# Seven block products in place of eight for five gate and up tile pairs of each feed-forward block

## The chip, the cores and the metric

The kernel runs on one core of a Trainium2 chip. The metric is the device time of the whole program in microseconds (us), the median of several executions; the profile shown is of one execution. TensorE is called PE here, VectorE DVE, ScalarE ACT, GpSimd POOL and SyncE SP.

## The reference

Two layers, each of a feed-forward network, a mixer (a recurrent group beside latent attention) and a second feed-forward network, over T = 528 tokens (16 meta tokens and 512 others) of 1024 features, all in 32 bit floats. The part that the change touches is the first half of the feed-forward network, D_FF = 2816:

```python
def swiglu(u, w_gate, w_up, w_down):
    return (jax.nn.silu(u @ w_gate) * (u @ w_up)) @ w_down
...
    for l in range(DEPTH):
        f = swiglu(rms_norm(h, ffn1_pre_g[l]), ffn1_w_gate[l], ffn1_w_up[l], ffn1_w_down[l])
        h = h + 0.5 * rms_norm(f, ffn1_post_g[l])
        ...
        f = swiglu(rms_norm(h, ffn2_pre_g[l]), ffn2_w_gate[l], ffn2_w_up[l], ffn2_w_down[l])
        h = h + 0.5 * rms_norm(f, ffn2_post_g[l])
    return h[:, N_META:]
```

## The kernel before

Features lie on the 128 partitions, tokens along the free axis. The program is six blocks, b = 0 to 5: blocks 0, 2, 3 and 5 are feed-forward blocks, 1 and 4 mixers. A feed-forward block has 22 pairs m, each of one gate tile and one up tile (128 columns of w_gate or w_up, 8 chunks of 128 rows: 128x1024 numbers), and then 8 output chunks of two w_down tiles (128x1408).

To keep 32 bit accuracy every operand is split into a high part (rounded to fp32r) and the rest: xh and xl of the tokens, whi and wlo of a weight tile. A product of a chunk is three matmuls, xh by whi, xl by whi, xh by wlo (`tile`, L1590), each once per half of the tokens (264 columns). A gate or up tile is thus 8 x 3 x 2 = 48 matmuls. In block 5 the meta tokens are no longer needed, and a tile from the pair m = 2 on is 24 matmuls of 512 columns.

A weight tile n goes through a ring of four places. SP loads it to `raw` once the low part of tile n - 4 has been made; ACT rounds it to `whi` (`hi`, L741) once PE has used tile n - 4; POOL subtracts (`lo`, L677, four instructions of 256 columns) to give `wlo`; PE waits for that (`slot_in`, L1600). Each engine works through its instructions in the order in which the code writes them.

The product of a tile stands in one of four pairs of PSUM banks, one bank for each half of the tokens; the pairs are taken in turn. For each m, `hidden` on DVE (L1297) scales the gate product from PSUM (L1301) and the up product (L1304), multiplies with the silu that ACT has made (L1308) and makes the low part of the hidden value (L1311); `hidden` on ACT (L913) makes the silu (L920), the high part of the hidden value (L924) and, between them, `hi` of two later tiles. Before the pair m = 0 stands a seam, in which the residual, the norm and xh, xl of the block are made, and `opening` on PE (L1618) takes the first three tiles half by half. The pairs are written as loops (`Fori`) on every engine.

Of the kernel before, what the change touches and what calls it, by code (L numbers as in the profile page):

```python
# [28 lines left out]
ALU = mybir.AluOpType  # L29
# [88 lines left out]

def build_program(nc, a, out, depth, d_ff):
# [6 lines left out]

    tiles = []
    slot0 = []
    for b in range(NB):
        slot0.append(len(tiles))  # L130
        tiles += MIX_TILES if b % 3 == 1 else [DC] * (2 * FC) + [FH] * (2 * DC)
    NSLOT = len(tiles)

# [5 lines left out]
    for b in range(NB):  # L139
        U[b, "post"] = U[b, "pre"] = n  # L140
        n += 1
        parts = MIX_UNITS if b % 3 == 1 else dict(gu=2 * FC, out=DC)
        for name, k in parts.items():
            U[b, name] = n
            n += k
    U[NB, "post"] = n

# [55 lines left out]
    def lo_made(n):  # L203

        return n + 1 + RING

# [21 lines left out]
    def out_slot(b, m):  # L228

        return slot0[b] + (S_OUT + m if b % 3 == 1 else 2 * FC + 2 * m + 1)  # L230
# [14 lines left out]
    with ExitStack() as ctx:  # L245
# [41 lines left out]
        hidl = sb_at("hidl", arena + FC * CH, [P, FC, T], F32R)  # L287

# [159 lines left out]
        lo_ready = sem("lo_ready")  # L448
        slots_used = sem("slots_used")
# [134 lines left out]

        def block_of(j):

            return (0, N_META) if j == 0 else (N_META + (j - 1) * P, P)
# [8 lines left out]
        def _(sp):  # L596
            def load(n, src, adv=0):

                sp.wait_ge(lo_ready, n + 1 + adv)
                k = tiles[n] * P  # L600
                sp.dma_start(raw[:, n % RING, 0:k], src).then_inc(raw_full[n % RING], 16)
# [20 lines left out]
            for b in range(NB):  # L622
                l, s0 = b // 3, slot0[b]
                if b % 3 == 1:
# [21 lines left out]
                    with sp.Fori(0, DC // 4) as j:  # L646
                        for m in range(4):
                            load(s0 + S_OUT + m, a["w_out"][l, j * 4 + m], j * 4)
                else:
# [3 lines left out]
                    with sp.Fori(1 if b == 0 else 0, FC // 2) as j:  # L653
                        for m in range(2):
                            load(s0 + 2 * m, a[name + "_gate"][l, j * 2 + m], j * 4)
                            load(s0 + 2 * m + 1, a[name + "_up"][l, j * 2 + m], j * 4)
                    with sp.Fori(0, DC // 2) as j:
                        for m in range(2):
                            for q in range(2):
                                load(s0 + 2 * FC + 2 * m + q, a[name + "_down"][l, j * 2 + m, q], j * 4)  # L660
# [15 lines left out]
        def _(pool):  # L676
            def lo(n, adv=0):  # L677

                pool.wait_ge(hi_ready, n + 1 + adv)
# [6 lines left out]

            def lo_run(first, last):

                n = first
                while n < last:  # L690
                    k = n
                    while k < last and tiles[k] == tiles[n] and (k in ARENA) == (n in ARENA):
                        k += 1
                    rounds = (k - n) // RING
                    if rounds > 1 and n not in ARENA:
                        with pool.Fori(0, rounds) as j:
                            for m in range(RING):
                                lo(n + m, j * RING)
                        n += rounds * RING
                    while n < k:  # L700
                        lo(n)
                        n += 1
# [15 lines left out]
            for b in range(NB):  # L718
                if b == 0:
                    pool.wait_ge(lo_ready, lo_made(RING - 2))  # L720
# [3 lines left out]
                lo_run(slot0[b] + RING, slot0[b + 1] if b + 1 < NB else NSLOT)  # L724
# [7 lines left out]
        def _(act):  # L732
# [8 lines left out]
            def hi(n, adv=0):  # L741
                if n < NSLOT:
                    r, k = n % RING, tiles[n] * P

                    if n in PREV:
                        act.wait_ge(slots_used, slot_used(PREV[n]) + adv)
                    act.wait_ge(raw_full[r], 16 * (n // RING + 1) + adv * 4)
# [161 lines left out]
            def ffn(b):  # L909
# [3 lines left out]
                def hidden(m, it=0):  # L913

                    adv = it * RING
                    ug = u0 + 2 * m
                    mm = m + 2 * it

                    act.wait_ge(psum_free[pair_of(ug)], read_out(ug) + it)
                    nc.scalar.activation(toks(tmp[2], trim), toks(tmp[0], trim), ACT.Silu).then_inc(silu_ready, 1)  # L920
                    if m > 0:
                        hi(s0 + 2 * m + RING, adv)
                    act.wait_ge(hid_ready, f0 + mm + 1)
                    nc.scalar.activation(toks(hidh[:, mm, :], trim), toks(tmp[3], trim),  # L924
                                         ACT.Copy).then_inc(hidh_ready, 1)
                    hi(s0 + 2 * m + 1 + RING, adv)

                hidden(0)
                hidden(1)
                with act.Fori(0, FC // 2 - 2) as j:  # L930
                    hidden(2, j)
                    hidden(3, j)
                hidden(FC - 2)
                hidden(FC - 1)
# [199 lines left out]
        def _(dve):  # L1134
# [96 lines left out]
            def first_seam():  # L1231

                def low(n, part):
# [3 lines left out]
                    else:  # L1237
                        dve.wait_ge(hi_ready, n + 1)
                    nc.vector.tensor_tensor(wlo[:, n, at], raw[:, n, at], whi[:, n, at].bitcast(F32), ALU.subtract)\  # L1239
                        .then_inc(first_lo if part == 0 else lo_ready, 1)  # L1240
# [52 lines left out]
            def ffn(b):  # L1293
# [3 lines left out]
                def hidden(m, it=0):  # L1297
                    adv, mm = it * RING, m + 2 * it
                    ug, uu = u0 + 2 * m, u0 + 2 * m + 1
                    dve.wait_ge(slots_used, slot_used(s0 + 2 * m) + adv)  # L1300
# [774 lines left out]
```

## Time and profile before

| | us |
|---|---|
| median of 3 runs | 2030.61 (2030.28 to 2030.77) |
| the profiled execution | 2030.33 |
| its span in the trace | 2028.5 |
| PE busy, matmuls | 2014.0 (99%) |
| PE busy, weight loads | 1927.0 (95%) |
| DVE busy | 697.2 (34%) |
| ACT busy | 747.9 (37%) |
| POOL busy | 997.4 (49%) |

The span is the time from the first to the last instruction that the profile shows; the execution's own time is 1.83 us more. Busy shares are means over stages that differ. Matmuls are pipelined: the time of one from start to end is over twice the time from one start to the next, so what a matmul costs is read from the distance of starts, not from its duration. Some matmul records can be missing.

### The profile page before, as it was taken

The numbers are of one execution on the slowest core, as the hardware profiler recorded it, in microseconds if no ns is written. First come the engines' busy times: TensorE is split into PE (matmuls) and PEld (weight loads), VectorE is DVE, ScalarE is ACT, GpSimd is POOL, SyncE is SP. The second block draws the span as 40 slices with busy tenths as digits, with TensorE's granted clock in tenths as the row PEclk, the third lists the DMA queues.
The fourth block names the chain that finished last, engine by engine and source line by source line (L and its number), as shares of the span: only waits on it lengthen the run. The fifth ranks groups of instructions, "written<-read, shape, count | busy, mean of one in ns | idle before, by whom it ended". The sixth has DMA issues, their size and how long they took to land.

```text
span 2028.5 us, 37353 instructions
## 1 busy us (share of the span) xinstructions
PE 2014.0 (99%) x15084; PEld 1927.0 (95%) x15084; DVE 697.2 (34%) x1093; ACT 747.9 (37%) x1210; POOL 997.4 (49%) x1257
## 2 busy tenths in 40 slices
PE   9999999999999999999999999999999999999998
PEld 8999999999899999999999999999998998888887
DVE  6222210378546222210062222103885462222102
ACT  5222222455556222232252222223555462232221
POOL 3544454475315544454374444544853155554542
PEclk9999999999999999999999999999999999999999
DMA  4322332222101322232122323321222013323321
GB/s 175 103 85 92 98 111 83 69 94 79 63 32 45 106 89 93 85 125 88 57 94 84 93 87 100 113 84 58 96 84 67 32 53 104 97 92 111 114 72 42
DMA packets 48415, 174.85 MB, mean 86 GB/s; under 512 B 5184, under 2 KB 9408, under 8 KB 48320
## 3 DMA queue, kind: packets, MB, share of 16 engines
q1 hardware_dynamic: 48176, 173.40, 26.1%
q8 instruction: 71, 1.16, 0.2%
q14 instruction: 24, 0.20, 0.0%
q10 hardware_dynamic: 144, 0.10, 0.0%
HBM read 171.38 MB, written 2.10 MB: 86 GB/s over the span
## 4 chain that ended last, share of the span: by engine, by line
PE 98%; DVE 1%; ACT 0%; DMA 0%; issue 0%; SPq 0%; DVEq 0%
PE ps L1588 97%; PE ps L1927 1%; DMA h<-in_x 0%; DVE osb L1535 0%; DVE xl L1545 0%; DVE tail_step L1205 0%; PE ps L1806 0%; ACT xh L778 0%; DVE probT L1503 0%; ACT prob L1061 0%; DVE small L1512 0%; DVE h L1210 0%; ACT tmp L1097 0%; ACT xh L1112 0%; DVE wlo L1239 0%
## 5 line engine op out<-in xcount | busy, mean ns | idle before, releaser
L683 POOL TENSOR_TENSOR wlo<-raw,whi 128x256 fp32r<-128x256 f32 (+2 forms) x1148 | 911.9, 826 | 787.4 <-ACT whi L748 787.4
L1588 PE MATMUL ps<-xh,whi 128*128 128x264 f32 (+2 forms) x3000 | 706.1, 298 | 3.2 <-DVE xl L1244 1.3
L1588 PE MATMUL ps<-xl,whi 128*128 128x264 f32 (+2 forms) x3000 | 703.0, 297 | 0.0
L1588 PE MATMUL ps<-xh,wlo 128*128 128x264 f32 (+2 forms) x3000 | 701.6, 297 | 0.0
L1588 PEld LDWEIGHTS ps<-xh,whi 128*128 128x128 f32 x3000 | 489.1, 188 | 21.0 <-DVE wlo L1239 2.3
L1588 PEld LDWEIGHTS ps<-xl,whi 128*128 128x128 f32 x3000 | 487.8, 188 | 14.8
L1588 PEld LDWEIGHTS ps<-xh,wlo 128*128 128x128 f32 x3000 | 487.5, 188 | 14.0
L748 ACT ACTIVATE whi<-raw 128x1024 fp32r<-128x1024 f32 (+2 forms) x289 | 321.4, 1114 | 152.5 <-PE ps L1588 152.4
L1588 PE MATMUL ps<-hidh,whi 128*128 128x264 f32 (+2 forms) x1276 | 313.6, 296 | 0.0
L1588 PE MATMUL ps<-hidh,wlo 128*128 128x264 f32 (+2 forms) x1276 | 312.3, 295 | 0.0
L1588 PE MATMUL ps<-hidl,whi 128*128 128x264 f32 (+2 forms) x1276 | 312.3, 295 | 0.0
L1588 PEld LDWEIGHTS ps<-hidl,whi 128*128 128x128 f32 x1276 | 214.2, 188 | 6.2
L1588 PEld LDWEIGHTS ps<-hidh,wlo 128*128 128x128 f32 x1276 | 213.8, 188 | 5.9
L1588 PEld LDWEIGHTS ps<-hidh,whi 128*128 128x128 f32 x1276 | 213.2, 188 | 6.1
L924 ACT ACTIVATE hidh<-tmp 128x528 f32 (+3 forms) x88 | 56.6, 643 | 412.7 <-DVE tmp L1308 412.7
L1304 DVE TENSOR_TENSOR tmp<-ps,rs_in 128x528 f32<-128x528 f32 (+1 forms) x88 | 61.9, 703 | 407.4 <-PE ps L1588 407.4
L1283 DVE TENSOR_TENSOR tmp<-tmp,tmp 128x264 f32<-128x264 f32 (+3 forms) x52 | 36.3, 698 | 413.5 <-ACT tmp L811 360.2
L920 ACT ACTIVATE tmp<-tmp 128x528 f32<-128x528 f32 (+1 forms) x88 | 56.6, 643 | 264.9 <-DVE tmp L1301 264.8
L1301 DVE TENSOR_TENSOR tmp<-ps,rs_in 128x528 f32<-128x528 f32 (+1 forms) x88 | 61.9, 704 | 218.7 <-PE ps L1588 203.8
L716 POOL TENSOR_TENSOR tmp<-tmp,tmp 128x264 f32<-128x264 f32 (+1 forms) x55 | 45.8, 833 | 103.1 <-ACT tmp L785 100.4
L1311 DVE TENSOR_TENSOR hidl<-tmp,hidh 128x528 f32 (+3 forms) x88 | 63.7, 723 | 80.9 <-ACT hidh L924 80.9
L683 POOL TENSOR_TENSOR w_mix<-raw,w_mix 128x256 fp32r<-128x256 f32 x32 | 25.5, 829 | 106.5 <-ACT w_mix L748 106.5
(192 smaller groups left out, 1685.9 us busy)
## 6 DMA issues: line engine op xcount, KB each, us to landing
raw<-in_ffn_up SPq DMA_DIRECT2D x88, 512.0 KB, 3.5
raw<-in_ffn_down SPq DMA_DIRECT2D x64, 704.0 KB, 4.1
raw<-in_ffn_gate SPq DMA_DIRECT2D x87, 512.0 KB, 3.5
raw<-in_w_in SPq DMA_DIRECT2D x28, 512.0 KB, 3.5
raw<-in_w_out SPq DMA_DIRECT2D x16, 512.0 KB, 3.5
raw<-in_w_q SPq DMA_DIRECT2D x8, 384.0 KB, 3.3
out_t<-h SPq DMA_DIRECT2D x16, 128.0 KB, 1.7
h<-in_x SPq DMA_DIRECT2D x2, 528.0 KB, 5.1
```

The source lines that it names most:

```text
L683: ins = nc.gpsimd.tensor_tensor(w_lo(n)[:, at], raw[:, r, at], w_hi(n)[:, at].bitcast(F32), ALU.subtract)
L716: nc.gpsimd.tensor_tensor(hs, hs, square_of(k, s, trim), ALU.add)\
L748: nc.scalar.activation(w_hi(n)[:, 0:k], raw[:, r, 0:k], ACT.Copy).then_inc(hi_ready, 1)
L920: nc.scalar.activation(toks(tmp[2], trim), toks(tmp[0], trim), ACT.Silu).then_inc(silu_ready, 1)
L924: nc.scalar.activation(toks(hidh[:, mm, :], trim), toks(tmp[3], trim), ACT.Copy).then_inc(hidh_ready, 1)
L1283: nc.vector.tensor_tensor(acc, acc, part(tmp[m % 2], trim), ALU.add).then_inc(sum_ready, 1)
L1301: nc.vector.tensor_tensor(halves(tmp[0], trim), unit(ug, trim, trim and m > 1), halves(rs_in, trim), ALU.mult).then_inc(psum_free[pair_of( ...
L1304: nc.vector.tensor_tensor(halves(tmp[1], trim), unit(uu, trim, trim and m > 0), halves(rs_in, trim), ALU.mult).then_inc(psum_free[pair_of( ...
L1311: nc.vector.tensor_tensor(toks(hidl[:, mm, :], trim), toks(tmp[3], trim), toks(hidh[:, mm, :], trim).bitcast(F32), ALU.subtract).then_inc( ...
L1588: return nc.tensor.matmul(o, w, x, start=start, stop=stop)
L1927: ins = nc.tensor.transpose(ps[:, c0:c0 + P], prob[e % 4][:, k0:k0 + P], ident)
```

## The change

For m = 5, 7, 9, 11 and 13 of each feed-forward block the gate tile G and the up tile U are taken together as a 2 x 2 matrix of blocks: rows gate and up, columns the lower and the upper four chunks of features; the tokens as a 2 x 2 matrix too, lower and upper features by first and second half of the tokens (B11, B12 / B21, B22). The product takes eight block products (four chunks by 264 tokens) in the kernel before; the change takes seven, by Winograd's form of Strassen's identity. In place of two weight tiles there are four in the ring: the gate as it is; `s13`, the sums S1 = Ur + Ul (r and l the upper and lower chunks) and S3 = Gl - Ul; `s2up`, S2 = S1 - Gl beside Ur; `s4`, S4 = Gr - S2, half a tile. DVE makes the sums in `raw` (L1443 to L1461 of the new kernel) from the two loaded tiles, ACT rounds each as before, and the low parts of the last three are made by DVE, those of the gate and of all other tiles by POOL.

The token sums T1 = B12 - B11, T2 = B22 - T1, T3 = B22 - B12, T4 = B21 - T2 are the same for all five pairs and are made once per block, while PE works on m = 1 to 4: for each of four chunks ACT scales two chunks of h to `t_in`, DVE makes four sums (`t_sums`), ACT rounds them to `t_hi` and DVE makes `t_lo` (128x1056 each). They lie where hidden values of later m will stand.

A changed pair uses three PSUM pairs: z, the gate's and the up's. ACT copies the first block product from z to SBUF (`part_copy`), so that its bank can be used again, and DVE adds the seven products up (`strassen_sums`, six additions of 264 columns). The loops over tiles are written out on all engines.

```diff
+STRASSEN = (5, 7, 9, 11, 13)
...
+            if m in STRASSEN:
+                for i, kind in enumerate(("gate", "s13", "s2up", "s4")):
+                    KIND[n + i] = kind
+                tiles += [DC, DC, DC, KH]
...
+    LO_DVE = {0, 1, 2} | {n for n in KIND if KIND[n] != "gate"}
...
+        def raw_reusable(eng, n):
+            if n >= RING:
+                wait_lo(eng, n - RING)
+                if KIND.get(n - RING) in ("gate", "s2up"):
+                    eng.wait_ge(w_sums, 3 * STRASSEN_N[n - RING] + 3)
```

On ACT:

```diff
+                for m in range(FC):
+                    n = TILES_OF[b, m]
+                    if m in STRASSEN:
+                        part_copy(m)
+                        for i in range(3):
+                            hi(n[i] + RING)
+                        silu(m)
+                        hi(n[3] + RING)
+                        hid_hi(m)
+                        continue
+                    silu(m)
+                    if m:
+                        hi(n[0] + RING)
+                    if m == 1:
+                        sum_hi(0)
+                        sum_inputs(1)
+                    hid_hi(m)
+                    hi(n[1] + RING)
+                    if 0 < m < 4:
+                        sum_hi(m)
+                    if m < 3 and m != 1:
+                        sum_inputs(0 if m == 0 else 3)
+                    elif m == 1:
+                        sum_inputs(2)
```

On DVE (`strassen_sums` is cut to its first three additions):

```diff
+                    if part == 0:
+                        dve.wait_ge(part_copied, q + 1)
+                        dve.wait_ge(slots_used, slot_used(n[0]))
+                        nc.vector.tensor_tensor(c11, x, c11, ALU.add).then_inc(part_added, 1)
+                    elif part == 1:
+                        dve.wait_ge(part_added, 6 * q + 1)
+                        dve.wait_ge(part_mm, 2 * q + 2)
+                        nc.vector.tensor_tensor(x, x, bank(z, trim, 1), ALU.add).then_inc(part_added, 1)
+                        dve.wait_ge(part_added, 6 * q + 2)
+                        dve.wait_ge(slots_used, slot_used(n[1]))
+                        nc.vector.tensor_tensor(y, x, bank(z, trim, 0), ALU.add).then_inc(psum_free[pair_of(z)], 1)
...
+                for m in range(FC):
+                    n = TILES_OF[b, m]
+                    nxt = [i + RING for i in n]
+                    sums(nxt[0])
+                    if m in STRASSEN:
+                        strassen_sums(m, 0)
+                        sums(nxt[1])
+                        low(nxt[0])
+                        sums(nxt[2])
+                        low(nxt[1])
+                        strassen_sums(m, 1)
+                        strassen_sums(m, 2)
+                        low(nxt[2])
+                        strassen_sums(m, 3)
+                        gate(m)
+                        up(m)
+                        sums(nxt[3])
+                        hid(m)
+                        low(nxt[3])
+                        hid_lo(m)
+                        continue
+                    gate(m)
+                    if m == 1:
+                        t_sums(0)
+                    elif 2 <= m <= 4:
+                        t_low(m - 1)
+                    sums(nxt[1])
+                    low(nxt[0])
+                    up(m)
+                    hid(m)
+                    low(nxt[1])
+                    hid_lo(m)
+                    if m == 1:
+                        t_low(0)
+                    if 1 <= m <= 3:
+                        t_sums(m)
+                    if b == 0 and m == FC - 4:
+                        decay_rates()
```

On PE, in `strassen`; `part` runs over four chunks k, three matmuls each:

```diff
+                        mm(o, wh, xhk, k == 0, False)
+                        mm(o, wh, xlk, False, False)
+                        ins = mm(o, wl, xhk, False, k == KH - 1)
...
+                slot_in(n[0])
+                part(n[0], False, tokens(0, a0), bank(z, trim, 0), ug).then_inc(part_mm, 1)
+                part(n[0], True, tokens(1, a0), bank(ug, trim, 0), uu).then_inc(slots_used, 1)
+                slot_in(n[1])
+                pe.wait_ge(t_lo_ready, KH * (b // 3 * 2 + b % 3 // 2) + KH)
+                part(n[1], False, sums(0), bank(uu, trim, 1))
+                pe.wait_ge(part_copied, q + 1)
+                part(n[1], True, sums(2), bank(z, trim, 0)).then_inc(slots_used, 1)
+                slot_in(n[2])
+                part(n[2], False, sums(1), bank(z, trim, 1)).then_inc(part_mm, 1)
+                part(n[2], True, sums(3), bank(uu, trim, 0)).then_inc(slots_used, 1)
+                slot_in(n[3])
+                part(n[3], False, tokens(1, a1), bank(ug, trim, 1), following).then_inc(slots_used, 1)
```

On PE, in the first changed pair of block 0: the last chunk of the second block product, and the beginnings of the two products of tile `s13` (a row is one matmul).

```order
L1803 MATMUL ps<-xh,whi 128x264 [waits psum_free1]
L1803 MATMUL ps<-xl,whi 128x264
L1803 MATMUL ps<-xh,wlo 128x264
L1803 MATMUL ps<-t_hi,whi 128x264 [waits t_lo_ready,lo_dve]
L1803 MATMUL ps<-t_lo,whi 128x264
...
L1803 MATMUL ps<-t_hi,wlo 128x264
L1803 MATMUL ps<-t_hi,whi 128x264 [waits part_copied]
L1803 MATMUL ps<-t_lo,whi 128x264
L1803 MATMUL ps<-t_hi,wlo 128x264
```

Twelve matmuls by token sums stand between the wait for `t_lo` and the wait for ACT's copy; from there the next product goes into the bank that was copied.

On ACT, one of the two pairs in the body of the loop before: silu, `hi`, high part of the hidden value, `hi`.

```order
L920 ACTIVATE tmp_67<-tmp_65 128x528 [waits psum_free3]
L746 REGISTER_ALU
L748 ACTIVATE whi<-raw 128x1024 [waits raw_full2,slots_used]
L923 REGISTER_ALU
L924 ISA [waits hid_ready]
L924 ACTIVATE hidh<-tmp_68 128x528
L746 REGISTER_ALU
L748 ACTIVATE whi<-raw 128x1024 [waits raw_full3,slots_used]
```

And in the kernel after, from the end of pair m = 4 to the end of m = 5 of block 0.

```order
L970 ACTIVATE tmp_67<-tmp_65 128x528 [waits psum_free1]
L799 ACTIVATE whi<-raw 128x1024 [waits w_sums,slots_used]
L974 ACTIVATE hidh<-tmp_68 128x528 [waits hid_ready]
L799 ACTIVATE whi<-raw 128x512 [waits w_sums,slots_used]
L998 ACTIVATE tmp_69<-ps 128x264 [waits part_mm]
L799 ACTIVATE whi<-raw 128x1024 [waits raw_full2,slots_used]
L799 ACTIVATE whi<-raw 128x1024 [waits raw_full3,slots_used]
L799 ACTIVATE whi<-raw 128x1024 [waits raw_full0,slots_used]
L970 ACTIVATE tmp_67<-tmp_65 128x528 [waits psum_free0]
L799 ACTIVATE whi<-raw 128x1024 [waits w_sums,slots_used]
L974 ACTIVATE hidh<-tmp_68 128x528 [waits hid_ready]
```

The copy from PSUM (L998) stands behind two `hi` and the high part of the hidden value of m = 4, and ahead of the three `hi` for the tiles that follow the changed pair.

On DVE, one of the two pairs in the body of the loop before.

```order
L1301 TENSOR_TENSOR tmp_65<-ps,rs_in 128x528 [waits slots_used]
L1303 REGISTER_ALU
L1304 TENSOR_TENSOR tmp_66<-ps,rs_in 128x528 [waits slots_used]
L1306 REGISTER_ALU
L1307 REGISTER_ALU [waits psum_free0]
L1308 TENSOR_TENSOR tmp_68<-tmp_67,tmp_66 128x528 [waits silu_ready]
L1311 ISA [waits hidh_ready]
L1311 TENSOR_TENSOR hidl<-tmp_68,hidh 128x528
```

And in the kernel after, from the scaling of the gate of m = 4 (L1395) to that of m = 5.

```order
L1395 TENSOR_TENSOR tmp_65<-ps,rs_in 128x528 [waits slots_used]
L1436 TENSOR_TENSOR t_lo<-t_sum,t_hi 128x1056 [waits t_hi_ready]
L1460 TENSOR_TENSOR raw<-raw 128x512 [waits w_sums,lo_ready]
L1468 TENSOR_TENSOR wlo<-raw,whi 128x1024 [waits hi_ready]
L1403 TENSOR_TENSOR tmp_66<-ps,rs_in 128x528 [waits slots_used]
L1411 TENSOR_TENSOR tmp_68<-tmp_67,tmp_66 128x528 [waits silu_ready,psum_free2]
L1468 TENSOR_TENSOR wlo<-raw,whi 128x512 [waits hi_ready]
L1416 TENSOR_TENSOR hidl<-tmp_68,hidh 128x528 [waits hidh_ready]
L1481 TENSOR_TENSOR ps<-tmp_69,ps 128x264 [waits slots_used,part_copied]
L1485 TENSOR_TENSOR tmp_69<-tmp_69,ps 128x264 [waits part_mm,part_added]
L1488 TENSOR_TENSOR tmp_69<-tmp_69,ps 128x264 [waits slots_used,part_added]
L1490 TENSOR_TENSOR tmp_69<-tmp_69,ps 128x264 [waits psum_free3]
```

Between the scaling of the gate and of the up product (L1395 and L1403) now stand the low part of token sums, a weight sum (L1460) and a low part of weights (L1468); behind them another low part and then the additions.

## Rows read from the trace of the kernel before

**Rows 1.** The page: span, and busy time by engine (share of it).

```profile
span 2028.5 us, 37353 instructions
...
PE 2014.0 (99%) x15084; PEld 1927.0 (95%) x15084; DVE 697.2 (34%) x1093; ACT 747.9 (37%) x1210; POOL 997.4 (49%) x1257
```

**Rows 2.** Waits of PE, the longest: waited for, us in total, times, longest.

```profile
PE ps L1585 <- DVE maskb L1136: 1.9, 1, 1.9
```

**Rows 3.** Timeline of DVE in block 2: start, us, instruction, [idle before <- releaser].

```profile
690.80 0.71 DVE L1301 TENSOR_TENSOR tmp<-ps,rs_in 128x528 f32<-128x528 f32 x1 [2.68 <-PE ps L1588]
...
708.42 0.71 DVE L1304 TENSOR_TENSOR tmp<-ps,rs_in 128x528 f32<-128x528 f32 x1 [5.17 <-PE ps L1588]
709.25 0.71 DVE L1308 TENSOR_TENSOR tmp<-tmp,tmp 128x528 f32<-128x528 f32 x1
...
796.52 0.71 DVE L1301 TENSOR_TENSOR tmp<-ps,rs_in 128x528 f32<-128x528 f32 x1 [2.66 <-PE ps L1588]
```

**Rows 4.** Timeline of DVE in block 5, where matmuls have 512 columns.

```profile
1678.52 0.69 DVE L1301 TENSOR_TENSOR tmp<-ps,rs_in 128x512 f32<-128x512 f32 x1 [2.11 <-PE ps L1588]
...
1711.88 0.69 DVE L1301 TENSOR_TENSOR tmp<-ps,rs_in 128x512 f32<-128x512 f32 x1 [2.39 <-PE ps L1588]
```

**Rows 5.** Timeline of PE in the openings of blocks 3 and 5.

```profile
1035.81 0.28 PE L1588 MATMUL ps<-xh,wlo 128*128 128x264 f32 x1
...
1042.39 0.29 PE L1588 MATMUL ps<-xh,wlo 128*128 128x264 f32 x1
...
1650.36 0.28 PE L1588 MATMUL ps<-xl,whi 128*128 128x256 f32 x1
...
1656.87 0.28 PE L1588 MATMUL ps<-xh,wlo 128*128 128x256 f32 x1
```

**Rows 6.** Timeline of PE in a mixer, and of ACT in the output of block 0.

```profile
423.79 0.28 PE L1588 MATMUL ps<-xh,wlo 128*128 128x264 f32 x1
...
439.82 0.41 PE L1588 MATMUL ps<-xh,wlo 128*128 128x264 f32 x2
...
300.83 0.61 ACT L811 ACTIVATE tmp<-ps 128x528 f32<-128x528 f32 x1 [6.65 <-PE ps L1588]
...
316.89 0.61 ACT L811 ACTIVATE tmp<-ps 128x528 f32<-128x528 f32 x1 [6.65 <-PE ps L1588]
```

**Rows 7.** Timeline of PE and ACT in block 2, at the end of a pair.

```profile
708.22 0.41 PE L1588 MATMUL ps<-xh,whi 128*128 128x264 f32 x2
...
710.10 0.65 ACT L924 ACTIVATE hidh<-tmp 128x528 f32 x1 [5.21 <-DVE tmp L1308]
710.65 1.05 ACT L748 ACTIVATE whi<-raw 128x1024 fp32r<-128x1024 f32 x1
```

**Rows 8.** Groups by form: line, engine, shapes, count | busy us, mean ns | idle before.

```profile
L826 ACT ACTIVATE f_mix<-ps,par 128x264 f32<-128x264 f32 x16 | 7.6, 477 | 0.0
...
L1187 DVE TENSOR_TENSOR tmp<-f_ffn,ps 128x264 f32<-128x264 f32 x48 | 19.7, 421 | 33.9 <-ACT ps L836 33.7
L1239 DVE TENSOR_TENSOR wlo<-raw,whi 128x1024 fp32r<-128x1024 f32 x2 | 2.4, 1222 | 0.5 <-ACT whi L748 0.5
L1239 DVE TENSOR_TENSOR wlo<-raw,whi 128x512 fp32r<-128x512 f32 x2 | 1.4, 692 | 0.5 <-ACT whi L877 0.5
```

**Rows 9.** Timeline of DVE and POOL, at the start of block 3 and in block 2.

```profile
1045.22 0.71 DVE L1301 TENSOR_TENSOR tmp<-ps,rs_in 128x528 f32<-128x528 f32 x1 [3.46 <-ACT rs_in L797]
...
1051.77 1.29 DVE L1308 TENSOR_TENSOR tmp<-tmp,tmp 128x528 f32<-128x528 f32 x1
...
1056.90 0.71 DVE L1301 TENSOR_TENSOR tmp<-ps,rs_in 128x528 f32<-128x528 f32 x1 [1.98 <-PE ps L1588]
...
1049.67 6.55 POOL L683 TENSOR_TENSOR wlo<-raw,whi 128x256 fp32r<-128x256 f32 x8 [2.62 <-ACT whi L748]
...
704.96 2.81 POOL L683 TENSOR_TENSOR wlo<-raw,whi 128x256 fp32r<-128x256 f32 x4 [2.10 <-ACT whi L748]
```

**Rows 10.** DMA issues: source, engine, count, size, us to landing.

```profile
raw<-in_ffn_up SPq DMA_DIRECT2D x88, 512.0 KB, 3.5
```

More of the change, by code:

```diff
@@ L645, in _ @@
                             sp.dma_start(ropet[0][:, :], a["rope"][0]).then_inc(rope0_in, 16)
-                    with sp.Fori(0, DC // 4) as j:
-                        for m in range(4):
-                            load(s0 + S_OUT + m, a["w_out"][l, j * 4 + m], j * 4)
+                    for m in range(DC):
+                        load(s0 + S_OUT + m, a["w_out"][l, m])
                 else:
@@ L685, in lo @@
                 ins.then_inc(lo_ready, 1)
[L687 to L702, printed above, removed]
             def seam(b):
@@ L723, in _ @@
                     seam(b)
-                lo_run(slot0[b] + RING, slot0[b + 1] if b + 1 < NB else NSLOT)
+                for n in range(slot0[b] + RING, slot0[b + 1] if b + 1 < NB else NSLOT):
+                    if n not in LO_DVE:
+                        lo(n)
             for i, k in enumerate(POOL_TAIL):
@@ L925, in hidden, with sum_inputs @@
                                          ACT.Copy).then_inc(hidh_ready, 1)
[L926 to L934, printed above, removed]
+                def sum_inputs(k):
+                    if k:
+                        act.wait_ge(t_sum_ready, KH * F + k)
+                    for i in range(2):
+                        c = k + i * KH
+                        ins = nc.scalar.activation(toks(t_in[:, i, :], trim), toks(h[:, c, :], trim), ACT.Copy,
+                                                   scale=col(g, b // 3, c))
+                    ins.then_inc(t_in_ready, 1)
@@ L1723, in ffn @@
                 product(u0 + 3, s0 + 3, tin, leads=True)
-                with pe.Fori(0, FC // 2 - 1) as j:
-                    for m in range(4):
-                        product(u0 + 4 + m, s0 + 4 + m, tin, adv=j * RING, it=j, led=True, leads=True)
+                for m in range(2, FC):
+                    n, following = TILES_OF[b, m], FIRST_U[b, m + 1]
+                    if m in STRASSEN:
+                        strassen(b, m, tin, following)
+                    else:
+                        product(GATE_U[b, m], n[0], tin, led=True, leads=True)
+                        product(UP_U[b, m], n[1], tin, led=True, leads=True, lead=following)
                 output(b, [(hidh[:, k, :], hidl[:, k, :]) for k in range(FC)])
```

259 lines of the change are left out of this document (198 added, 61 removed).

## The prediction

> **What bounds the kernel now.** I read the page first: PE is busy 99% of the span the other engines under 50% [rows 1]. Then the waits of PE: even the longest is only 1.9 us, once, for a mask made at the program's start [rows 2]. So the gate and up stretches run at the pace of the matmuls, and a matmul less is worth one distance between starts. That is read on DVE, which scales the gate product once per pair: 690.80 to 796.52 us are nine pairs, 11.747 us each, 96 matmuls at 0.1224 us [rows 3]. In block 5 three pairs take 1678.52 to 1711.88 us, 11.12 each, 48 matmuls of 512 columns at 0.2317 us [rows 4].
>
> **What it removes.** A changed pair is 7 products x 4 chunks x 3 = 84 matmuls in place of 96; in block 5, 84 of 256 columns in place of 48 of 512. The pattern of a changed pair, one token half after the other with three matmuls per chunk, stands already in the openings: 54 steps in 6.58 us, 0.1219 us each at 264 columns, and 55 steps in 6.51 us, 0.1184 at 256 [rows 5]. So halving the columns of block 5 costs little: two of 256 cost 0.2368 against 0.2317 for one of 512.
>
> A changed pair has nine waits on PE (four tiles, token sums, the copy, three PSUM leads) where two tiles had four. What a wait that is met costs isn't shown alone. From above: 48 matmuls of the pairs take 5.87 us, and 48 in the output, where 132 take 16.06 us [rows 6], would take 5.84; the 0.03 us may be the two waits of a tile, 0.017 each, or nothing. I take 0.017, five more being 0.08 us a pair; below, 0.
> - Blocks 0, 2, 3, 15 pairs: 84 x 0.1219 + 0.08 = 10.32 us, so 1.43 less each, 21.4 us.
> - Block 5, 5 pairs: 84 x 0.1184 + 0.08 = 10.03, so 1.09 less each, 5.5 us.
>
> Together 26.9 us, if nothing on PE waits longer.
>
> **What it adds, and what hides it.** I call X the start of PE's first matmul of a changed pair. From the end of an ordinary pair in block 2: PE goes on at 708.22, DVE's up at 708.42, hid at 709.25 [rows 3], ACT's high part at 710.10 and its next at 710.65 [rows 7]; that is X + 0.2, 1.03, 1.88, 2.43. Next on ACT is now `hi` of s4, 512 columns, about as long as the high part of 528: 0.65 us, the next starting after 0.55 [rows 7]. So the copy from PSUM starts at X + 2.98 and, at 0.48 us (the scaled copy of 264 columns) [rows 8] and 0.1 us for the signal, is known to PE at about X + 3.55. PE wants it after 36 matmuls, X + 4.39 (X + 4.26 in block 5). This is the tightest hand-over: 0.8 us to spare. Queued behind it on ACT are the three `hi` of the next tiles, which PE needs from X + 10.3.
>
> The first of them can round at X + 3.5 to 4.5, POOL makes its low part in 2.8 us [rows 9], so it is ready by X + 7.5. The next waits for its ring place (X + 5.9) and is ready at X + 10.2, wanted at X + 16.2; the following gate at X + 13, wanted at X + 22.
>
> DVE adds six times, about 0.42 us each as the instruction of 264 columns with one operand in PSUM [rows 8]; the last can start after the pair, X + 10.5. Then gate, up, two sums into s13 (0.69 each), hid, a low part (1.22) and hidl: done near X + 17. The ordinary pair brings two sums, the gate and the low part of s2up, done near X + 21.4; up falls due at X + 22.2. So DVE enters the next changed pair with 0.8 us to spare, and is busy some 14 us of 22 (six additions 2.5, eight old instructions 5.7, four sums 2.8, three low parts 3.1), against 5.7 in two pairs before. A late DVE delays up, hid, ACT and the copy in this order, so PE waits only when DVE is more than 0.8 + 0.8 = 1.6 us late. PSUM: each pair of banks is read 5 us or more before PE wants it, z's of the next changed pair 11 us.
>
> SP: a load now also waits for the sums that read its place. The up tile of the next changed pair is loaded when POOL has made a low part at X + 7.4 and lands 3.5 us later [rows 10], X + 11; DVE wants it at X + 12.2. The bytes are the same. POOL makes three low parts in two pairs where it made four; it was no bound.
>
> Token sums, once per block beside m = 1 to 4: in block 3, from DVE's first gate at 1045.22 and its third at 1056.90 (PE's own pace) [rows 9], PE begins m = 5 at 1056.90 + 5 x 5.87 = 1086.2. DVE has to do until then four pairs (10.6 us at 0.66), 16 sums (1.8 us per chunk of four alone, up to 3.8 with POOL in the way), four low parts of 1056 columns (1.25), and 6.5 us for the weights and the gate of m = 4: 29 to 37 us in 41, with waits for ACT in between. Laid out by hand in queue order, the token sums' last low part ends at 1084 (wanted X + 2.9 = 1089) and the low part of s2up at 1086. Just in time: I take a stall of 0, and up to 3 us a block as the upper end.
>
> The port: DVE's hid took 1.29 us where POOL was subtracting and 0.71 otherwise [rows 3, 9]. The Trainium skill, "SBUF — State Buffer", in its section on which instructions contend, says that a DVE instruction with two SBUF inputs and a GpSimd one that reads SBUF lock each other out for a whole instruction; the trace agrees (1.29 = 0.71 + most of one POOL instruction of 0.70). By that rule the new weight and token sums can each lose 0.6 us beside POOL, the six additions (one operand in PSUM) nothing. It bears on the two sums into s13 at X + 12.2, where POOL runs until X + 13, and on the token sums, as counted above. Near X itself POOL rests, since both tiles that come are DVE's.
>
> The loops written out: I take 0. The mixer, already written out, has 131 matmuls of 264 columns in 16.03 us [rows 6], 0.1224 each, just the pace of the loops. "Runtime: NRT & Kernel Launch" in the Trainium skill, on instruction fetch, says that a taken branch breaks the sequential prefetch and can stall; by it the ten iterations of four blocks would give time back. The trace shows no such stall.
>
> The decay rates, small DVE instructions once in the program, move to m = 18 of block 0, where DVE idles 5.17 us before up and 2.68 before gate in each pair [rows 3]: nothing.
>
> **Sum.** 2028.5 - 26.9 = 2001.6 us of span, 2003.4 us with the 1.83 us around it. The median of the runs is 0.28 above the profiled execution: **2003.7 us**. Own range of this case: 2001.5 (no cost of waits, steps of 0.1217) to 2006.5.
>
> **Rivals.**
> - *Late preparation* (chance 0.17). The token sums and the first weight sums end after X in each block, by 2 to 3 us above the margin. For it: DVE has 29 to 37 us of work in 41, twice it waits for ACT per chunk. Against it: the margin of 1.6 us. Four blocks x 1 to 3 us: 2007 to 2015.
> - *Hand-over in each changed pair* (0.09). The copy comes late again and again, as DVE's work between the pairs runs beside POOL. 0.2 to 1.3 us x 20: 2008 to 2030.
> - *Slower* (0.04). The same place with a price above 26.9 / 20 = 1.34 us a pair. It needs DVE 1.6 + 1.34 = 2.9 us later than laid out, five instructions with 0.58 us lost each (1.29 against 0.71). Only the two sums into s13 and what follows them to X + 13 can meet POOL, by my layout; if POOL runs later than I think, low parts and sums of the next ordinary pair do too. From there 2031 to 2040.
> - *More than forecast* (0.05). Branches or register instructions of the loops cost PE something that goes: 0.065 us a pair (96 matmuls at 0.1224 against 0.1217) in all 88 pairs, 5.7 us: 1997 to 2001.
> - *Not seven products in effect* (0.01). If a matmul of the new order did not overlap its weight load as in the openings, the pair would cost 96 steps again: no change, 2030. The openings speak against it.
>
> **Chances and range.** The forecast has 0.64. Of the 0.26 of the two late cases 0.16 lies below 2012. The range 2001.0 to 2012.0 holds 0.8. A measurement of this kernel tells 0.2%, 4 us, from no change. Faster by more: all cases but the slower one, the one without effect and the worst of the hand-over, 0.94; within 0.2%: 0.02; slower: 0.04.
>
> **What would show it.** Right: 84 matmuls a changed pair, which leaves PE's count at 15084 [rows 1], as block 5 gains (5 x 36) what the other blocks lose (15 x 12); DVE's scaling of gates 22.0 us apart over a changed and an ordinary pair (10.3 + 11.75), 21.15 in block 5; PE's waits for ACT's copy and for t_lo at or near 0; DVE near 14 us busy per 22. Late preparation would show as one wait of PE per block, in m = 5; the hand-over as twenty waits for ACT's copy line. Wrong altogether: steps of over 0.125 us in the changed pairs, or waits of PE for DVE's low parts.

## The result, and the profile after

| | before | after |
|---|---|---|
| median of the runs, us | 2030.51 | 2001.81 (2001.66 to 2001.96) |
| span of the profiled execution, us | 2028.5 | 1999.9 |
| PE busy, us (matmuls) | 2014.0 (15084) | 1986.1 (15084) |
| DVE busy, us | 697.2 | 935.5 |
| ACT busy, us | 747.9 | 824.9 |
| POOL busy, us | 997.4 | 969.5 |

The ratio of the times is 0.9859, with a 95% interval of 0.9842 to 0.9876. The change takes 28.6 us off the span, where 26.9 were forecast; the time is 2001.8 us, where 2003.7 was forecast.

The page of the kernel after, span and busy times, to be laid beside [rows 1]:

```profile
span 1999.9 us, 35639 instructions
...
PE 1986.1 (99%) x15084; PEld 1909.3 (95%) x15084; DVE 935.5 (47%) x1453; ACT 824.9 (41%) x1318; POOL 969.5 (48%) x1177
```

PE has as many matmuls as before, as the forecast counted (15 x 12 less, 5 x 36 more), and is as full. DVE has 238 us more to do and POOL 28 less; PE, busy 99%, stays the bound. The waits of PE after, the whole list (waited for, us in total, times, longest), beside [rows 2]:

```profile
PE ps L1800 <- DVE maskb L1226: 1.7, 1, 1.7
PE ps L1803 <- DVE xl L1334: 1.2, 2, 0.8
PE ps L1803 <- DVE wlo L1329: 0.9, 1, 0.9
PE ps L1803 <- DVE xl L1761: 0.8, 3, 0.4
PE ps L1803 <- ACT tmp L998: 0.6, 1, 0.6
PE ps L2063 <- DVE xl L1761: 0.5, 1, 0.5
```

One of twenty changed pairs, the first of block 5, makes PE wait for ACT's copy of the first block product (L998). The list says 0.6 us, but the spans of matmuls overlap; the starts show more. With it stands the scaling of the up product of m = 4 (L1403), late at X + 2.07 of this pair (X = 1682.77), where it comes at X + 0.2 in most; ACT's copy is queued behind what hangs on it:

```profile
1684.83 0.69 DVE L1403 TENSOR_TENSOR tmp<-ps,rs_in 128x512 f32<-128x512 f32 x1
...
1686.90 0.28 PE L1803 MATMUL ps<-t_hi,wlo 128*128 128x256 f32 x1
1687.76 0.39 PE L1803 MATMUL ps<-t_hi,whi 128*128 128x256 f32 x1 [0.57 <-ACT tmp L998]
```

By its 84 starts this pair takes 10.72 us and each of the other four of block 5 9.87, so the wait costs 0.85 us. The list of before has one wait that is gone from the list of after, in the mixer of block 4:

```profile
PE ps L1588 <- DVE qt L1416: 0.9, 1, 0.9
```

Now the pace, from DVE's scaling of the gate product (L1395) in block 2 and block 5, answering [rows 3, 4]: start, us, instruction.

```profile
722.09 0.71 DVE L1395 TENSOR_TENSOR tmp<-ps,rs_in 128x528 f32<-128x528 f32 x1
...
744.07 0.71 DVE L1395 TENSOR_TENSOR tmp<-ps,rs_in 128x528 f32<-128x528 f32 x1
...
805.19 0.71 DVE L1395 TENSOR_TENSOR tmp<-ps,rs_in 128x528 f32<-128x528 f32 x1 [3.00 <-PE ps L1803]
816.94 0.71 DVE L1395 TENSOR_TENSOR tmp<-ps,rs_in 128x528 f32<-128x528 f32 x1 [3.00 <-PE ps L1803]
...
1694.14 0.69 DVE L1395 TENSOR_TENSOR tmp<-ps,rs_in 128x512 f32<-128x512 f32 x1
...
1715.15 0.69 DVE L1395 TENSOR_TENSOR tmp<-ps,rs_in 128x512 f32<-128x512 f32 x1
```

From one changed pair to the next are 21.98 us, of which a plain pair still takes 11.75 (805.19 to 816.94; 11.745 over several). So a changed pair takes 10.235 us and saves 1.51. In block 5 they are 21.01 us apart, 9.89 for the changed pair, 1.23 saved. 15 x 1.51 + 5 x 1.23 = 28.8 us. Less the wait of 0.85, with the 1.05 us of the mixer's wait that is gone (by the starts of the matmuls around it) and less 0.4 us by which DVE's first gate comes later at the program's start, that is 28.6 us.

The hand-over that the forecast called the tightest, in block 2: PE starts its second changed pair, m = 7, at X = 711.20. The timelines of PE, DVE, ACT and POOL in turn:

```profile
711.20 0.28 PE L1803 MATMUL ps<-xh,whi 128*128 128x264 f32 x1
...
711.40 0.71 DVE L1403 TENSOR_TENSOR tmp<-ps,rs_in 128x528 f32<-128x528 f32 x1 [1.08 <-PE ps L1803]
712.14 0.71 DVE L1411 TENSOR_TENSOR tmp<-tmp,tmp 128x528 f32<-128x528 f32 x1
...
721.62 0.44 DVE L1498 TENSOR_TENSOR ps<-tmp,ps 128x264 f32<-128x264 f32 x1 [0.69 <-PE ps L1803]
...
723.33 0.68 DVE L1451 TENSOR_TENSOR raw<-raw 128x512 f32<-128x512 f32 x1
723.92 1.23 DVE L1452 TENSOR_TENSOR raw<-raw 128x512 f32<-128x512 f32 x1
...
712.88 0.65 ACT L974 ACTIVATE hidh<-tmp 128x528 fp32r<-128x528 f32 x1 [3.83 <-DVE tmp L1411]
713.43 0.62 ACT L799 ACTIVATE whi<-raw 128x512 fp32r<-128x512 f32 x1
713.96 0.37 ACT L998 ACTIVATE tmp<-ps 128x264 f32<-128x264 f32 x1
714.32 1.06 ACT L799 ACTIVATE whi<-raw 128x1024 fp32r<-128x1024 f32 x1
...
715.46 9.14 POOL L747 TENSOR_TENSOR wlo<-raw,whi 128x256 fp32r<-128x256 f32 x12 [12.84 <-ACT whi L799]
```

The copy stands at X + 2.76 to 3.13 (laid out: 2.98 to 3.46), PE wants it at X + 4.39. DVE had been idle 1.08 us when its up product came (laid out: 0.8). Of the two sums into s13, L1451 takes 0.68 us and L1452 1.23, while POOL is subtracting until 724.60: L1451 got in ahead of POOL's last instruction, which took 1.22 us in place of 0.73, and L1452 stood behind that one.

### The profile page after: what moved, and what is told of

It is laid out like the page before. It is cut to its first block, busy times and chain, and to the rows that moved or that the text cites. A ratio compares the mean times of both kernels' runs of the same rounds, so it can differ in the third digit from the quotient of the medians.

```text
span 1999.9 us, 35639 instructions
## 1 busy us (share of the span) xinstructions
PE 1986.1 (99%) x15084; PEld 1909.3 (95%) x15084; DVE 935.5 (47%) x1453; ACT 824.9 (41%) x1318; POOL 969.5 (48%) x1177
## 4 chain that ended last, share of the span: by engine, by line
PE 96%; DVE 2%; ACT 1%; issue 0%; DMA 0%; DVEq 0%; SPq 0%; ACTq 0%
PE ps L1803 95%; PE ps L2184 1%; DMA h<-in_x 0%; ACT whi L799 0%; DVE osb L1751 0%; ACT xh L829 0%; ACT t_in L983 0%; DVE t_sum L1430 0%; DVE t_sum L1431 0%; DVE t_sum L1429 0%; DVE xl L1761 0%; ACT t_hi L990 0%; DVE tail_step L1295 0%; DVE t_sum L1428 0%; DVE tmp L1411 0%
## 5 line engine op out<-in xcount | busy, mean ns | idle before, releaser
L1803 PE MATMUL ps<-xh,whi 128*128 128x264 f32 (+2 forms) x2680 | 645.1, 296 | 2.9 <-DVE xl L1334 1.2
L1803 PE MATMUL ps<-xl,whi 128*128 128x264 f32 (+2 forms) x2680 | 641.4, 295 | 0.0
L1803 PE MATMUL ps<-xh,wlo 128*128 128x264 f32 (+2 forms) x2680 | 640.4, 295 | 0.0
L1803 PEld LDWEIGHTS ps<-xh,whi 128*128 128x128 f32 x2680 | 444.7, 188 | 17.1 <-DVE wlo L1329 2.0
L799 ACT ACTIVATE whi<-raw 128x1024 fp32r<-128x1024 f32 (+3 forms) x329 | 356.0, 1083 | 253.6 <-PE ps L1803 224.4
L1803 PEld LDWEIGHTS ps<-xl,whi 128*128 128x128 f32 x2680 | 443.5, 188 | 11.4
L1803 PEld LDWEIGHTS ps<-xh,wlo 128*128 128x128 f32 x2680 | 443.4, 188 | 10.5
L974 ACT ACTIVATE hidh<-tmp 128x528 fp32r<-128x528 f32 (+1 forms) x88 | 56.2, 639 | 234.6 <-DVE tmp L1411 234.5
L1403 DVE TENSOR_TENSOR tmp<-ps,rs_in 128x528 f32<-128x528 f32 (+1 forms) x88 | 61.6, 699 | 173.8 <-PE ps L1803 173.8
L1395 DVE TENSOR_TENSOR tmp<-ps,rs_in 128x528 f32<-128x528 f32 (+1 forms) x88 | 61.7, 701 | 97.9 <-PE ps L1803 82.2
L1803 PE MATMUL ps<-t_hi,whi 128*128 128x264 f32 (+1 forms) x320 | 90.5, 283 | 0.6 <-ACT tmp L998 0.6
L1803 PE MATMUL ps<-t_lo,whi 128*128 128x264 f32 (+1 forms) x320 | 90.5, 283 | 0.0
```

The lines of the kernel that those rows point to most:

```text
L799: nc.scalar.activation(w_hi(n)[:, 0:k], raw[:, r, 0:k], ACT.Copy).then_inc(hi_ready, 1)
L974: nc.scalar.activation(toks(hidh[:, m, :], trim), toks(tmp[3], trim), ACT.Copy).then_inc(hidh_ready, 1)
L1395: nc.vector.tensor_tensor(halves(tmp[0], trim), unit(ug, trim, trim and m > 1 and m not in STRASSEN), halves(rs_in, trim), ALU.mult).then_ ...
L1403: nc.vector.tensor_tensor(halves(tmp[1], trim), unit(uu, trim, trim and m > 0 and m not in STRASSEN), halves(rs_in, trim), ALU.mult).then_ ...
L1803: return nc.tensor.matmul(o, w, x, start=start, stop=stop)
```

## The experiments

The kernel before, measured again beside each group of experiments, has medians of 2030.33 to 2030.51 us; times of different groups are thus comparable to about 0.2 us.

### Is it the pairs, or the loops that were written out?

```diff
-STRASSEN = (5, 7, 9, 11, 13)
+STRASSEN = ()
-                    if m == 1:
-                        t_sums(0)
-                    elif 2 <= m <= 4:
-                        t_low(m - 1)
```

and the rest of the token sums taken out likewise.

> No pair is changed and no token sums are made; only the loops over the tiles are written out, as in the changed kernel. Theory (the gain is the fewer and shorter matmul steps of the changed pairs): the time of before, 2030.5 us within 1 us, and 11.747 us a pair as in the loops. Rival (the loops themselves cost 0.065 us a pair, which would explain that the change brought 28.6 us and not the forecast 26.9): 2024.8 us, 11.68 us a pair.

Measured: 2030.73 us (ratio to before 1.0001, interval 0.9992 to 1.0011). The gate scalings of block 2:

```profile
703.07 0.71 DVE L1385 TENSOR_TENSOR tmp<-ps,rs_in 128x528 f32<-128x528 f32 x1 [3.00 <-PE ps L1785]
714.81 0.71 DVE L1385 TENSOR_TENSOR tmp<-ps,rs_in 128x528 f32<-128x528 f32 x1 [3.00 <-PE ps L1785]
```

11.74 us a pair, as in the loops. The rival "more than forecast" falls: writing the loops out brings nothing, so the gain comes with the changed pairs.

```diff
-STRASSEN = (5, 7, 9, 11, 13)
+STRASSEN = (9,)
```

> Only the pair m = 9 of each block is changed, the token sums are made as in the changed kernel. Read from the trace after, a changed pair saves 11.747 - 10.235 = 1.51 us in blocks 0, 2 and 3, and 11.12 - 9.89 = 1.23 us in block 5. Theory: the gain is proportional to the pairs, 3 x 1.51 + 1.23 = 5.8 us, so 2024.7 us. Rival (part of the gain does not come with the pairs but with the rest of the edit): a gain above 8 us with one pair.

Measured: 2024.42 us (2023.78 to 2024.54; ratio 0.9969, interval 0.9958 to 0.9981), 6.0 us less than the 2030.45 beside it. The token sums and all else that comes with one pair cost nothing that shows, and pairs pay one by one. (From block 2's first gate scaling to block 3's are 1.52 us less than before, the price of one pair; the mixer's wait of 0.9 us is gone here too.)

### What does a wait cost that is met?

```diff
                 for k in range(DC):
+                    if k:
+                        slot_in(n)
                     if leads and k == DC - 1:
```

> The changed kernel with a wait before each of the chunks 1 to 7 of an ordinary tile, for the same weights that the tile has already waited for, so each is met: 146 tiles x 7 = 1022 more waits on PE. The forecast priced a met wait at 0.017 us at most: 17.4 us more, 2019 us. If a met wait costs PE nothing: 2001.8 us. The trace after, where a changed pair with nine waits has steps of 0.1218 us and a plain tile 0.1224, speaks for nothing.

Measured: 2001.9 us (2001.86 to 2002.12), where 17.4 us more were due at the forecast's price. 1022 more waits move the median by 0.1 us, within the spread of the runs. The 0.08 us a pair of the forecast was no cost of waits.

### Then why is a step 0.1218 us in a changed pair and 0.1224 in a plain one?

The ordinary tiles in the order of the changed pairs, all matmuls of the first half of the tokens and then those of the second:

```diff
-                for k in range(DC):
+                for i, grp in enumerate(groups(trim, trim)):
+                    for k in range(DC):
...
-                    ins = tile(u, n, k, xh[:, k, :], xl[:, k, :], groups(trim, trim), k == 0, k == DC - 1)
+                        ins = tile(u, n, k, xh[:, k, :], xl[:, k, :], [grp], k == 0, k == DC - 1)
```

> The changed kernel with the ordinary tiles worked one token half after the other, as the openings and the changed pairs do, in place of both halves for each chunk. Theory A (the order of halves makes the 0.0006 us between a step of 0.1224 in plain tiles and 0.1218 in changed pairs): 115 tiles x 48 x 0.0006 = 3.3 us less, 1998.5 us, and 11.69 us a plain pair. Theory B (it is something else): 2001.8 us.

Measured: 1997.98 us (1997.89 to 1998.26; ratio 0.984, interval 0.9824 to 0.9856). Three plain pairs of block 2:

```profile
791.39 0.71 DVE L1395 TENSOR_TENSOR tmp<-ps,rs_in 128x528 f32<-128x528 f32 x1 [0.92 <-PE ps L1803]
...
826.47 0.71 DVE L1395 TENSOR_TENSOR tmp<-ps,rs_in 128x528 f32<-128x528 f32 x1 [2.97 <-PE ps L1803]
```

35.08 / 3 = 11.693 us, a step of 0.1218, that of the changed pairs in the kernel after. The edit of the order makes the difference, and this is a version faster than both kernels. But a step isn't set by the order within its own pair alone. The changed pairs, whose code this edit leaves as it was, went from 10.22 to 10.16 us by the starts of their 84 matmuls, and in the kernel after itself the same 84 take 10.17 us in the first changed pair of blocks 0, 2 and 3 (689.27 to 699.44 in block 2) and 10.22 in the others. To see whether each change of PSUM bank costs, every second pair of matmuls is turned:

```diff
-                    for t0, nt, c0 in grp:
+                    for t0, nt, c0 in grp[::-1] if (3 * t + i) % 2 else grp:
```

> The changed kernel with the two halves of the tokens in turned order for every second matmul pair of a tile (first, second, second, first, ...), so that PE changes the PSUM bank half as often in ordinary tiles. One half after the other took 3.8 us off (1998.0 us). Theory A (each change of bank between matmuls costs): half of it, 1999.9 us, and 11.72 us a plain pair. Theory B (it is how many matmuls of one half stand in a row at the tile's start or end, or the place of the last wait): 2001.8 us, 11.747 us a pair.

Measured: 1999.85 us (1999.68 to 2000.1), just what theory A gave. But its parts don't agree with it. Plain pairs in block 2, and output chunks (L862) in block 0, whose matmuls were turned too:

```profile
792.37 0.71 DVE L1395 TENSOR_TENSOR tmp<-ps,rs_in 128x528 f32<-128x528 f32 x1 [0.90 <-PE ps L1803]
...
827.49 0.71 DVE L1395 TENSOR_TENSOR tmp<-ps,rs_in 128x528 f32<-128x528 f32 x1 [2.98 <-PE ps L1803]
...
276.90 0.61 ACT L862 ACTIVATE tmp<-ps 128x528 f32<-128x528 f32 x1 [6.66 <-PE ps L1803]
293.02 0.61 ACT L862 ACTIVATE tmp<-ps 128x528 f32<-128x528 f32 x1 [6.66 <-PE ps L1803]
```

A plain pair is 35.12 / 3 = 11.707 us, which is 0.038 of the 0.052 us that whole halves bring, not half; and an output chunk became slower, 16.12 us against 16.06 [rows 6], with half as many changes of bank. A price per change of bank is thus not the rule; that the total fits it is luck, more gained in the tiles and something lost in the outputs. That the order counts is shown; what in it counts stays open.

### How near is the hand-over?

```diff
-                        part_copy(m)
-                        for i in range(3):
-                            hi(n[i] + RING)
+                        hi(n[0] + RING)
+                        part_copy(m)
+                        for i in range(1, 3):
+                            hi(n[i] + RING)
```

> The changed kernel with ACT's copy of the first block product behind one more rounding (that of the tile n + 4, for which ACT must wait until PE has used tile n). Theory (the hand-over of the copy is the tightest and has about 1.1 us to spare: in the trace after the copy ends 3.1 us into the pair and PE wants it at 4.4): the rounding starts at 3.1, the copy at 4.1 and is known at 4.6, so PE waits 0.2 us in each of 20 pairs: 2004 to 2009 us in all, and the trace names ACT's copy as what PE waits for, 20 times. Rival (PE's queue of started matmuls hides so short a wait): 2001.8 us.

Measured: 2007.59 us (2007.35 to 2009.25; ratio 0.989, interval 0.9873 to 0.9906), 5.8 us slower than after. Waits of PE's weight loads and of its matmuls:

```profile
PEld ps L1804 <- ACT tmp L998: 5.4, 20, 2.0
...
PE ps L1804 <- ACT tmp L998: 1.8, 1, 1.8
```

Twenty waits for the copy, shown on the weight loads; on the matmuls only the longest shows, since their spans overlap. So a list of matmul waits hides waits of some 0.2 us. By the starts, a changed pair takes 10.45 us in place of 10.22, in block 5 10.14 in place of 9.87, and the first of block 5, which waited already, takes 11.93 in place of 10.72. The twentyfold place of the rival "hand-over in each changed pair" is real, and the unaltered order clears it by about 1.1 us (copy done at X + 3.13; the weight load of the matmul that wants it starts at X + 4.27).

### Does the late start of the token sums cost?

```diff
-STRASSEN = (5, 7, 9, 11, 13)
+STRASSEN = (6, 8, 10, 12)
```

> Four changed pairs per block, m = 6, 8, 10, 12, so that the token sums have one more ordinary pair of time. By the price of a pair (1.51 and 1.23 us) 2001.8 + 5.8 = 2007.6 us if the token sums are no burden in the changed kernel, less the one wait of 0.6 us that the trace after shows in block 5: 2007.0 us, and no wait of PE for ACT's copy. Rival (late preparation costs the changed kernel more than that wait shows, up to 3 us a block): 1998 to 2005 us.

Measured: 2007.49 us (2007.33 to 2007.71), and in the trace no wait for L998. That is 0.5 us above the 2007.0 that was due, and the trace has a wait that makes up for it, the one that before has in the mixer of block 4 and after has not:

```profile
PE ps L1803 <- DVE qt L1632: 0.9, 1, 0.9
```

Block by block there is no burden left to find: from block 2's first gate scaling to block 3's are 389.60 us before, 383.55 here (four pairs, 6.05 less) and 381.96 after (five, 7.64 less), 1.51 and 1.53 a pair. So "late preparation" costs the changed kernel the wait in block 5, 0.85 us, and nothing in the other blocks.

### Who makes the low parts?

```diff
-    LO_DVE = {0, 1, 2} | {n for n in KIND if KIND[n] != "gate"}
+    LO_DVE = {0, 1, 2}
```

> The changed kernel with the low parts of the tiles s13, s2up and s4 made by POOL, in four instructions each, in place of DVE. Theory (everything but PE has room in these stretches): 2001.8 us, with DVE busy about 60 us less. Rival (port: POOL would now subtract around the start of a changed pair, where DVE makes the hidden value, and delays it by 0.6 us and more, which the copy's margin of 1.1 us does not take twice): up to 1 us in each of 20 pairs, 2003 to 2020 us.

Measured: 2001.54 us (2000.77 to 2001.93), no slower than after. The expected fall of DVE's busy time was wrong: 935.5 to 913.8 us, 22 in place of 60. The low parts that left DVE had taken 63 us, and by the durations of the others, those with two operands in SBUF that stayed take 34 us more (durations overlap at their ends, so the three don't add up exactly). Where it went, in block 2 (timelines of DVE and POOL):

```profile
701.87 2.08 DVE L1451 TENSOR_TENSOR raw<-raw 128x512 f32<-128x512 f32 x1
703.87 0.68 DVE L1452 TENSOR_TENSOR raw<-raw 128x512 f32<-128x512 f32 x1
704.47 0.70 DVE L1411 TENSOR_TENSOR tmp<-tmp,tmp 128x528 f32<-128x528 f32 x1
...
699.84 3.56 POOL L747 TENSOR_TENSOR wlo<-raw,whi 128x256 fp32r<-128x256 f32 x5
```

A sum of 512 columns takes 2.08 us while POOL runs back to back, and the next one of the same size 0.68 once POOL has stopped (703.40). Much of the work taken from DVE and given to POOL came back to DVE as waiting beside POOL. The rival's delay is there as well: in the second changed pair of block 2 ACT's copy starts at X + 3.32 in place of X + 2.76. It was hidden because the copy's margin covers it.

### Neighbours

```diff
-STRASSEN = (5, 7, 9, 11, 13)
+STRASSEN = (5, 7, 8, 10, 11, 13)
```

> Six changed pairs in each block, m = 5, 7, 8, 10, 11, 13, so that two pairs of them are neighbours. Each more pair saves 5.8 us if all is hidden: 1996.0 us. Theory (two neighbours leave DVE too little time, its additions, sums and low parts of one changed pair come to more than 10.2 us, and ACT's copy stands behind the high part of the hidden value): the second of two neighbours waits 1.5 us or more for the copy, 8 times: 2002 to 2012 us, slower than with five pairs. Rival (the distance between changed pairs does not matter): 1996.0 us.

Measured: 2024.37 us (2023.64 to 2026.02; ratio 0.9971, interval 0.9958 to 0.9983). The direction was foreseen, the size not: 28.4 us above the 1996.0 of six hidden pairs, 3.5 us for each of eight neighbourhoods, not 1.5. What PE waited for, and DVE in the first of two neighbours in block 2:

```profile
PE ps L1803 <- DVE tmp L1395: 11.0, 8, 1.8
PE ps L1803 <- ACT tmp L998: 5.6, 9, 0.7
...
721.87 0.43 DVE L1481 TENSOR_TENSOR ps<-tmp,ps 128x264 f32<-128x264 f32 x1
722.21 1.09 DVE L1451 TENSOR_TENSOR raw<-raw 128x512 f32<-128x512 f32 x1
723.23 1.22 DVE L1452 TENSOR_TENSOR raw<-raw 128x512 f32<-128x512 f32 x1
724.48 1.12 DVE L1455 TENSOR_TENSOR raw<-raw 128x512 f32<-128x512 f32 x1
725.63 1.64 DVE L1468 TENSOR_TENSOR wlo<-raw,whi 128x1024 fp32r<-128x1024 f32 x1
727.19 0.41 DVE L1485 TENSOR_TENSOR tmp<-tmp,ps 128x264 f32<-128x264 f32 x1
```

Between the first addition and the second (L1481, L1485) now stand three sums and a low part for the neighbour, each drawn out by POOL, 5.0 us together. The second addition starts 5.3 us behind the first, where it was 3.5 in the kernel after. The gate product is scaled late, and PE, which wants that PSUM pair for the neighbour's up product, waits up to 1.8 us each time. The forecast of this run counted the copy alone. To see what DVE's load and the copy's place have to do with it:

```diff
-    LO_DVE = {0, 1, 2} | {n for n in KIND if KIND[n] != "gate"}
+    LO_DVE = {0, 1, 2}
...
+                        if m + 1 in STRASSEN:
+                            part_copy(m + 1)
                         hid_hi(m)
```

with the copy taken from the head of its own pair; behind an ordinary pair too it goes ahead of the high part of the hidden value.

> The same six pairs, with the low parts of the tiles s13, s2up and s4 on POOL, and ACT's copy of the first block product ahead of the high part of the hidden value of the pair before. If DVE's load and the copy's place are what neighbours cost: 1996 to 1999 us. If neighbours wait for something else (raw tiles, PSUM): as without these two edits, 2002 us or more.

Measured: 2013.99 us (2013.91 to 2014.82), 10.4 us better than without the two edits and still 12.2 worse than five pairs apart, so between the two values that were expected. PE now waits first for POOL's low parts:

```profile
PE ps L1806 <- POOL wlo L747: 5.3, 8, 0.9
PE ps L1806 <- DVE tmp L1398: 2.3, 5, 0.6
PE ps L1806 <- ACT tmp L998: 1.8, 5, 0.4
```

DVE's load and the copy's place were parts of the price. The rest is spread over POOL's low parts, the PSUM pairs and the copy, so I don't put it down to one cause. In this layout the two versions with neighbouring pairs are slower than five pairs apart.

### A better version

The halves one after the other, and the copy ahead of the high part of the hidden value:

> Five changed pairs, ordinary tiles worked one half after the other, and ACT's copy of the first block product moved ahead of the high part of the hidden value and one rounding. Theory: the copy's margin grows from 1.1 us to over 2, and the one wait of 0.6 us in block 5 goes: 1997.4 us. Rival (ACT then stands waiting for PE's first product and delays the high part, which DVE and the next steps take badly): 1998 to 2000 us.

Measured: 1997.24 us (1997.15 to 1997.72; ratio to before 0.9837, interval 0.9824 to 0.9851). The copy now ends at X + 2.05, and the wait for it is gone from the trace: the first changed pair of block 5 takes 9.87 us in place of 10.72. Against 1997.98 us for the halves alone the time is 0.7 us less, which by the ranges of the runs (1997.89 to 1998.26) is just clear and fits those 0.85. It is the fastest of all versions, 4.6 us below the changed kernel.

## Why the prediction was right, step by step

- **What bounds the kernel.** Right: the pace of the matmuls, before and after, with one new wait of 0.85 us and one of 1.05 gone.
- **What a changed pair takes.** The mechanism was right, the size a little off: 10.235 us, not 10.32; 9.89 in block 5, not 10.03. The mis-sized term is the five more waits at 0.017 us, 1.6 us of the 1.7 by which the gain was underrated; they cost nothing that could be measured. The difference between tiles and output [rows 6], from which that price was taken, is not in the waits; the order of the token halves changes it, by a cause that stays open. That a price "may be the waits, or nothing" was said, and the wrong end was taken. The steps of the openings, 0.1219 and 0.1184 [rows 5], became 0.1218 and 0.1177. Without that term the sum would have been 28.5 us, and that this is so near the 28.6 is in part luck: 0.3 us more from the shorter steps of block 5, the 1.05 us of the mixer's wait that is gone, the new wait of 0.85 and the later start of 0.4 were in no sum, and they all but cancel.
- **Halving the columns in block 5.** Right: it still saves, 1.23 us a pair against 1.09 forecast.
- **The hand-over of the copy.** Laid out for X + 3.46, found at X + 3.13. It is hidden as it stands, and with one rounding put ahead of it PE waits in every changed pair.
- **DVE's load.** The last addition was laid out for X + 10.5 and starts at X + 10.42; DVE is idle 1.08 us, not 0.8, before the next changed pair. It is busy 14.15 us of 21.98 there; some 14 of 22 were laid out.
- **The token sums, just in time.** Right for three blocks. In block 3 PE starts the pair at X = 1071.23; the token sums' last low part ends at X - 1.2 (laid out: X - 2.2) and DVE scales the up product at X + 0.41 in place of X + 0.2, which the margin covers. In block 5, where PE is fastest, DVE comes to it 1.87 us late, more than the copy's margin (0.8 us as laid out, 1.1 as found), and PE waits 0.85 us. "Late preparation" took place once, just below the 1 to 3 us of that rival.
- **The port.** Right: only instructions with two operands in SBUF were drawn out, a sum of 512 columns to 1.23 us here and 2.08 in the run that gives POOL more; the additions with an operand in PSUM stayed at 0.43 beside a busy POOL. In which of them are drawn out this is as the Trainium skill has it ("SBUF — State Buffer", "Who interferes with whom"). "Slower" needed five such hits before each changed pair; from 711.20 to 733.18 there is one (L1452), which ends 8 us ahead of PE's next changed pair.
- **The loops.** Right: nothing. The Trainium skill ("Runtime: NRT & Kernel Launch", "Instruction fetch mechanics") says that a taken branch stalls when its target isn't in the stretch already fetched. No such stall shows here: 2030.73 us with the loops over tiles written out, 2030.45 with them.

## What to carry to other kernels

When PE is the bound and its waits are near 0, an algorithm with fewer products pays just its share of steps, as long as the side work is laid out in queue order against PE's clock and every hand-over keeps a margin: write down each as "ready at X + a, wanted at X + b". A side engine at half load can still be the limit over a short stretch: two changed pairs in a row took back more than the sixth pair saved. And waits on PE that are already met cost nothing to speak of here; look at the order of the matmuls first. Read a hand-over that costs a few tenths of a microsecond from the starts of matmuls or from the weight loads, since the list of matmul waits shows too little of it or nothing.

## What the runs showed of the hardware

- 1022 more waits on PE that were met already moved the median by 0.1 us (2001.9 against 2001.81).
- With the order of two token halves in different PSUM banks a step of 264 columns changed by 0.5 ns: 11.745 us against 11.693 for 96 matmuls. Changed pairs whose own code was the same took 10.17 or 10.22 us. In the output chunks turning every second pair of matmuls cost, 16.12 against 16.06 us, where in the tiles it gained. The cause is open.
- A DVE sum of 512 columns with two SBUF operands went from 0.68 to 2.08 us beside a POOL that subtracts back to back, which is more than one POOL instruction of about 0.7 us in its way. It goes the other way too: POOL's 0.73 us became 1.22 behind a DVE sum that started just before it.
- A wait that cost PE 0.85 us stood as 0.6 in the list of matmul waits, and in the run with one rounding ahead of the copy nineteen of about 0.2 us did not stand there at all.
